# Norm scales applied to products, an earlier start of the recurrence, and tanh gates in a two-block transformer kernel

## Chip, cores and metric

One core of a Trainium2 chip runs the whole program. The metric is the device time of one execution in microseconds (us). The engines are named as in the profile: PE is TensorE, DVE is VectorE, ACT is ScalarE, POOL is GpSimd, SP issues DMAs.

## What is computed

512 tokens of width 1024 pass through a first block (two attentions, gates, an output product `o1`, a final RMS norm) and then a second block of two layers. The change touches the seam of the blocks and layer 0 of the second one:

```python
x = rms_norm(h + merged @ w_out, final_norm_gain)           # end of the first block
h = rms_norm_2(x, mix_norm_g[0]);  z = h @ hg_w_in          # mixer norm, columns q | f | i | g | qm
mem_n = rms_norm_2(mem, mem_norm_g[l])                      # 256 memory rows, l = 0 and 1
kv = mem_n @ w_mem_kv[l];  k = rms_norm_2(kv[..., :256]);  q = rms_norm_2(qm)
m = softmax(q @ k.T * scale) @ kv[..., 256:]                # memory attention, 4 heads
o = hgrn2(q, f, i)                                          # recurrence, 6 heads of 128
o = rms_norm_2(o, onorm_g) * silu(g)                        # per head
x = x + concat([o, m]) @ w_out[0]                           # then the feed-forward of layer 0
```

## The kernel before

The tokens lie along the free axis: `X[:, k, :]` is feature tile k (of 8) for all 512 tokens. Every dense product is split in high and low halves (`XH`, `XL`; weights `WH`, `WL`), three 512-column matmuls for each of 8 k-tiles, 24 for one job. A job is a 128x1024 weight slab or several. The order of jobs is fixed in `plan_stream` (line 90 on) and each engine has its whole program written out in that order, tied by semaphores. A slab goes through three engines: SP brings it to `RAW` (a ring of 4), ACT rounds it to `WH` (`high`, L1104), POOL subtracts to get `WL` (`low`, L541). `WH` and `WL` have two slots (`SPLIT = 2`): `split_past(name)` on ACT issues `high` for the slab two after the named job's, and has to wait until that job is done. Four PSUM banks `DB[0..3]` take the jobs' results in turn, and each is emptied by ACT or DVE, as the plan says.

Around the change the work runs in this order:

- `zb0..7`, `pab0..7`: the gates and branch products. ACT evacuates `zb`, DVE forms the merged tiles `MH`, `ML`.
- `o1_0..7`: the first block's output product. DVE adds each to `X` and squares and sums it (`add_to_x`, L1575 to L1580). Between them memory is loaded to `MRAW` and its norm runs on DVE and ACT (`norm(1, ...)`): 16 tiles of 256 columns are multiplied by gain and root (L1544), rounded (ACT L1143) and subtracted (L1548) into `XH`, `XL`. All of it stands in DVE's order between `o1_3` and `o1_4`.
- `norm_sum(2)`: PE sums the squares of the finished `X`; root; DVE multiplies the 8 tiles of `X` by gain and root (L1763). `norm_sum(3)` and `norm_high(3)` are the mixer norm of the same `X`: squares, root, 8 more tiles of multiply, round and subtract. Memory keys and values (`mk00, mk01, mv0, mk10, mk11, mv1`, 256 columns) are in between.
- `qm00, qm01` (queries of the memory attention), `hf0..5` (forget gates, ACT sigmoid, then a block of six Ln), `hq0..5` (Silu), with the scans of the decays on DVE (L1790, L1791) as soon as the Ln are done.
- Memory attention `m0`: 8 pairs of steps with `hv0`, `hv1` (the values of the recurrence) as pieces beside. DVE makes row minima (L1668), ACT the Exp (L1191), PE transposes, ACT copies to `PT` (L1201), PE multiplies by values.
- The recurrence: for each head h, 7 levels (POOL makes differences L576, L577; ACT Exp L1379; DVE `weigh` L1822; PE L912; DVE `place`), an exact diagonal and two block steps, then PE L939. The job `hg{h}` (the output gate's column tile) is cut in 8 pieces laid beside levels 1 to 8. ACT copies it out (`evac`), and does Silu for four heads after head 4 and for two at the end (`gates_done`, L1369).
- The outputs' RMS norm: squares by ACT (L1361), sums in groups `hoa` (heads 0 to 3) and `hob` (4 and 5), root, `head_spread` by PE (L693), `output_made` and `output_low` by DVE, `output_high` by ACT. Heads 0 to 2 lie within head 5's levels, heads 3 to 5 behind the recurrence, before `wo00`.
- `tail(0, ...)`: `wo00..7` and the feed-forward. Here a norm already goes the other way: `late_tile` (ACT L1148 to L1150) and `late_low` (DVE L1586, L1590) write the halves of the unscaled sum times gain, and the root multiplies products later.

Of the kernel before, what the change touches and what calls it, by code (L numbers as in the profile page):

```python
# [15 lines left out]
P = 128  # L16
# [15 lines left out]
HG = 6  # L32
# [35 lines left out]
def plan_stream():  # L68
# [50 lines left out]
    for k in range(HG):  # L119
        add(f"hg{k}", 1, 1, KD, "act", (0,))  # L120
# [38 lines left out]
SQB = {0: 0, 1: KD, 3: 2 * KD}  # L159
ACC = {0: 0, 1: KD - 1, 2: 2 * (KD - 1), 3: 2 * KD - 1, 4: 3 * KD - 2, 5: 3 * KD - 1, 6: 3 * KD}  # L160

XLB = {0: 0, 1: KD, 3: 3 * KD}
LATE = {4: 0, 5: KD, 6: 2 * KD}


def plan_heads():
# [3 lines left out]
    for group, names, parts, m, nt in (("mk", [f"mk{l}{k}" for l in range(2) for k in range(2)], 1, 2, MEM // P),  # L170
                                       ("qm0", ["qm00", "qm01"], 1, 2, NT), ("hoa", [f"ho{h}" for h in range(4)], 1, 1, NT), ("hob", ["ho4", "ho5"], 1, 1, NT),
# [15 lines left out]
XTB = XLB  # L187
WO0 = [6, 7, 0, 1, 2, 3, 4, 5]
# [10 lines left out]
def build(nc, stream, xt_in, memt_in, pars, convp, consts, rope_tabs, toep, masks8, resets, cz_in, pos_in, out):  # L199
    with ExitStack() as ctx:  # L200
# [62 lines left out]
        MRAW = at("MRAW", [P, KD, MEM], A0 + 0)  # L263
# [62 lines left out]
        SUMS_AT = {"mk": (SC[0], 0), "qm0": (SC[0], 16), "hoa": (TB, 16), "hob": (TB, 32), "cq": (SC[0], 0), "ckv": (SC[0], 4),  # L326
# [45 lines left out]
        x_new = sem("x_new")  # L372
# [47 lines left out]
        hg_silu = sem("hg_silu")  # L420
# [116 lines left out]
        def _(pool):  # L537
# [20 lines left out]
            lows(JOBS["za7"].done + SPLIT, s0 + 2)  # L558

            pool.wait_ge(decays_ready, 1)  # L560
            for h in range(HG):
                b = HB[:, h, :]
                for l in range(8):
# [18 lines left out]
                    if h and l == 1:  # L582
                        low((s0 + h + 1) % RING, s0 + h + 1)
# [5 lines left out]
        def _(pe):  # L589
# [106 lines left out]
            def norm_sum(q, n=TOK):  # L696

                pe.wait_ge(acc_done, ACC[q] + (KD - 1 if q in SQB else 1))
                sum_cols(SC[0], PB[:, 0 if q in SQB else 2, 0:n], ONES[:, 0:1]).then_inc(ss_done, 1)

            def norm_spread(q, n=TOK):
                pe.wait_ge(rs_ready, q + 1)
                spread(SC[1], RS[:, 0:n]).then_inc(rs_spread, 1)
# [51 lines left out]
            def head_sum(group, a, part=0):  # L755
# [7 lines left out]
                sq = (TMP[:, a % 2, :] if group in ("hoa", "hob") else square_at(idx))[:, 0:P * nt]  # L763
# [1445 lines left out]
```

## Time and profile before

| | us |
|---|---|
| median of 3 runs | 1872.19 (1869.97 to 1872.7) |
| profiled execution | 1874.77 |
| its span, first to last instruction | 1873.0 |
| PE busy in it | 1747.3 (93%) |
| DVE / ACT / POOL busy | 893.0 / 760.1 / 699.6 |

The profiled execution is 2.6 us above the median. PEclk is the clock granted to TensorE as a share of 2.4 GHz: 0.50 is 1.2 GHz. A matmul's start is recorded, its end is modelled, so two neighbours overlap in the rows. "idle before" in brackets is the time in which the engine had nothing to do, and what ended it.

### The profile page before, as it was taken

The page shows a single profiled execution, that of the slowest core. Times are in us where ns is not written, and L with a number is a line of the kernel's source. Part 1 is how long each engine was busy: PE and PEld are TensorE (multiplying, and loading weights), DVE is VectorE, ACT ScalarE, POOL GpSimd, SP SyncE. Part 2 cuts the span into 40 slices and gives each one's busy share as a digit, 9 for nine tenths or more (in the row PEclk, how much of TensorE's full clock was granted, in tenths as well). Part 3 has the DMA queues.
Part 4 walks back from the last instruction along what each step waited for, and adds up shares of the span by engine and source line. Part 5 has one row for each costly group of instructions (what it writes and reads, how often), then busy time and mean ns, then how long its engine had stood idle before and what let it go on. Part 6 is the DMA issues. An engine that isn't in the chain of part 4 may idle for free.

```text
span 1873.0 us, 24838 instructions
## 1 busy us (share of the span) xinstructions
PE 1747.3 (93%) x8605; PEld 1420.2 (76%) x8605; DVE 893.0 (48%) x1675; ACT 760.1 (41%) x1167; POOL 699.6 (37%) x362
## 2 busy tenths in 40 slices
PE   5999899998689989889999999998887999999999
PEld 4778566887668778778888888887755788888887
DVE  3587565457534236554555541143454355555200
ACT  4333455323335424444545443324423354444322
POOL 2344211443333346514444444543300244444444
PEclk9999899999789979899999999999988899999999
DMA  4233211232222211012323233332200123332333
GB/s 178 84 108 101 63 40 35 90 111 92 79 67 90 79 45 35 23 34 91 101 90 100 90 101 106 108 96 68 74 5 1 56 91 94 97 101 90 101 106 118
DMA packets 43278, 151.75 MB, mean 81 GB/s; under 512 B 4929, under 2 KB 5057, under 8 KB 43073
## 3 DMA queue, kind: packets, MB, share of 16 engines
q1 hardware_dynamic: 41184, 145.16, 24.7%
q10 hardware_dynamic: 2016, 5.53, 0.9%
q8 instruction: 51, 0.84, 0.2%
q14 instruction: 27, 0.21, 0.0%
HBM read 148.58 MB, written 2.10 MB: 80 GB/s over the span
## 4 chain that ended last, share of the span: by engine, by line
issue 53%; POOL 23%; PE 21%; DVE 1%; ACT 1%; DMA 1%; POOLq 1%; ACTq 0%; DVEq 0%
POOL WL L541 22%; PE DB L617 4%; PE DB L618 3%; PE DB L619 3%; PE SC L912 2%; PE SC L717 1%; PE DB L742 1%; PE OB L731 1%; PE TB L617 1%; PE DB L731 1%; DMA CONST<-in_consts_dram 1%; PE TB L618 0%; PE TB L619 0%; PE DB L669 0%; PE DB L667 0%
## 5 line engine op out<-in xcount | busy, mean ns | idle before, releaser
L541 POOL TENSOR_TENSOR WL<-RAW,WH 128x1024 fp32r<-128x1024 f32 x268 | 643.5, 2401 | 1161.4 <-ACT WH L1104 1161.4
L1104 ACT ACTIVATE WH<-RAW 128x1024 fp32r<-128x1024 f32 x268 | 283.7, 1059 | 731.5 <-PE DB L619 307.0
L617 PE MATMUL DB<-XH,WH 128*128 128x512 f32 (+1 forms) x616 | 256.2, 416 | 11.7 <-DVE XL L1548 6.5
L972 PE MATMUL DB<-XH,WH 128*128 128x512 f32 x640 | 249.0, 389 | 0.0
L973 PE MATMUL DB<-XL,WH 128*128 128x512 f32 x640 | 249.0, 389 | 0.0
L974 PE MATMUL DB<-XH,WL 128*128 128x512 f32 x640 | 249.0, 389 | 0.0
L618 PE MATMUL DB<-XL,WH 128*128 128x512 f32 (+1 forms) x616 | 243.8, 396 | 0.0
L619 PE MATMUL DB<-XH,WL 128*128 128x512 f32 (+1 forms) x616 | 243.1, 395 | 0.0
L617 PEld LDWEIGHTS DB<-XH,WH 128*128 128x128 f32 x616 | 120.6, 196 | 51.0 <-issue 19.1
L619 PEld LDWEIGHTS DB<-XH,WL 128*128 128x128 f32 x616 | 120.6, 196 | 24.9
L972 PEld LDWEIGHTS DB<-XH,WH 128*128 128x128 f32 x640 | 120.1, 188 | 25.1
L973 PEld LDWEIGHTS DB<-XL,WH 128*128 128x128 f32 x640 | 120.1, 188 | 24.9
L974 PEld LDWEIGHTS DB<-XH,WL 128*128 128x128 f32 x640 | 120.1, 188 | 24.8
L991 PE MATMUL DB<-GH,WH 128*128 128x512 f32 x352 | 136.9, 389 | 0.0
L992 PE MATMUL DB<-GL,WH 128*128 128x512 f32 x352 | 136.9, 389 | 0.0
L993 PE MATMUL DB<-GH,WL 128*128 128x512 f32 x352 | 136.9, 389 | 0.0
L618 PEld LDWEIGHTS DB<-XL,WH 128*128 128x128 f32 x616 | 120.9, 196 | 20.5 <-issue 1.2
L1914 DVE TENSOR_TENSOR DB<-DB,SQ 128x512 f32<-128x512 f32 x88 | 61.2, 695 | 42.0 <-PE DB L974 41.2
L993 PEld LDWEIGHTS DB<-GH,WL 128*128 128x128 f32 x352 | 66.1, 188 | 13.7
L991 PEld LDWEIGHTS DB<-GH,WH 128*128 128x128 f32 x352 | 66.1, 188 | 13.7
L992 PEld LDWEIGHTS DB<-GL,WH 128*128 128x128 f32 x352 | 66.1, 188 | 13.6
L1201 ACT ACTIVATE PT<-DB 128x512 f32<-128x512 f32 (+3 forms) x52 | 35.8, 688 | 99.7 <-PE DB L742 99.7
(398 smaller groups left out, 2916.9 us busy)
## 6 DMA issues: line engine op xcount, KB each, us to landing
RAW<-in_stream_dram SPq DMA_DIRECT2D x268, 512.0 KB, 3.5
TP<-in_toep_dram ACTq DMA_DIRECT2D x4, 512.0 KB, 3.7
out_dram<-X SPq DMA_DIRECT2D x8, 256.0 KB, 4.4
X<-in_xt_dram SPq DMA_DIRECT2D x4, 256.0 KB, 5.2
X<-in_xt_dram ACTq DMA_DIRECT2D x4, 256.0 KB, 5.6
MRAW<-in_memt_dram ACTq DMA_DIRECT2D x1, 1024.0 KB, 6.2
CONST<-in_consts_dram ACTq DMA_DIRECT2D x1, 448.0 KB, 9.9
MSKI<-in_masks_dram ACTq DMA_DIRECT2D x1, 288.0 KB, 3.5
```

The costliest lines, as they stand in the source:

```text
L541: nc.gpsimd.tensor_tensor(WL[:, s, :], RAW[:, j, :], WH[:, s, :].bitcast(F32), ALU.subtract).then_inc(lo_done, 1)
L617: mm(o, WH[:, s, c], hi(k), start=(k == 0), stop=False)
L618: mm(o, WH[:, s, c], lo(k), start=False, stop=False)
L619: last = mm(o, WL[:, s, c], hi(k), start=False, stop=(k == job.kts - 1))
L972: mm(o, WH[:, s, c], xh(k), start=(k == 0), stop=False)
L973: mm(o, WH[:, s, c], xl(k), start=False, stop=False)
L974: last = mm(o, WL[:, s, c], xh(k), start=False, stop=(k == KD - 1))
L991: mm(o, WH[:, s, c], GH[:, k, :], start=(k == 0), stop=False)
L992: mm(o, WH[:, s, c], GL[:, k, :], start=False, stop=False)
L993: last = mm(o, WL[:, s, c], GH[:, k, :], start=False, stop=(k == FF - 1))
L1104: A(WH[:, n % SPLIT, :], RAW[:, n % RING, :], ACT.Copy).then_inc(hi_done, 1)
L1914: V.tensor_tensor(DB[j], DB[j], SQ[:, 0, :], ALU.mult).then_inc(scaled, 1)
```

## The change

1. The final norm, the mixer norm and the memory norms no longer multiply tiles. Memory (`MRAW`, now in the space of `SB` and `PT`) is loaded at the end of the first attention, and squared and summed during `zb`/`pab`. Its halves `MXH`, `MXL` (own space) are memory times gain, without the root, and are made between the `o1` jobs. The keys take the root in DVE (`ROOTM`), the values in ACT's evacuation as a scale.
2. `o1` jobs end in `late_tile`/`late_low` with gain `GAIN2` (final gain times mixer gain): per tile 4 ACT instructions, a DVE addition, a DVE subtract and two DVE additions into `TB` and `OB` (two sums of squares). The roots of both norms are formed from the two sums with a chain of small instructions; `ROOT2` multiplies each product of `qm`, `hf`, `hq`, `hg` on DVE in its bank (`root_scaled`); the values take it as a scale.
3. The scan of head k stands behind `root_scaled("hq{k}")` on DVE; ACT's Silu of `hq` waits for it too. The fill of `PT`, the `decays_ready` signal and POOL's first levels come before or inside the memory attention; the first Exp of head 0 stands in ACT's order just before the last copy to `PT` (`values_and_first_level`). The last group of memory outputs is left for DVE to finish within head 0.
4. The gate is `tanh(0.5 z)` on ACT, and `(tanh + 1) * z` on DVE, one head later; the factor 0.5 is in the norm's gain. Pieces of `hg` lie beside levels 2, 3, 4, 5, 6, 7, 7, 8.
5. Output norms in three groups: heads 0 to 2, 3 and 4, and 5. `wo00` and `wo01` are run in pieces, with the spreads and sums of heads 3 to 5 between the pieces.

The diff, cut to its core ("..." marks what is left out):

```diff
-XLB = {0: 0, 1: KD, 3: 3 * KD}
-LATE = {4: 0, 5: KD, 6: 2 * KD}
+LATE = {2: 0, 4: KD, 5: 2 * KD, 6: 3 * KD}
+SPREAD_AT = [(4, 6), (5, 3), (5, 8)]
+GATE_AT = [2, 3, 4, 5, 6, 7, 7, 8]
...
             pool.wait_ge(decays_ready, 1)
+            pool.wait_ge(exp_done, segments["m0"][-1][1]["g"] + 1)
...
-                    if h and l == 1:
-                        low((s0 + h + 1) % RING, s0 + h + 1)
+                    if l == 1:
+                        low((s0 + h + (h > 0)) % RING, s0 + h + (h > 0))
+                    if h == 0 and l == 4:
+                        low((s0 + 1) % RING, s0 + 1)
...
             for k in range(2):
                 feature_job(f"mk0{k}", *memory_halves(0), n=MEM, xready=XLB[1])
+            norm_sum(2)
+            norm_sum(3)
             token_job("mv0", *memory_halves(0), MEM, tiles=2)
...
+            pe.wait_ge(std_done, 4)
+            for a in range(2):
+                head_sum("mk", a)
             token_job("mv1", *memory_halves(1), MEM, tiles=2)
             pe.drain().then_inc(arena_free, 1)
-            pe.wait_ge(x_new, KD)
+            norm_spread(2)
             norm_spread(3)
...
+                if final is not None:
+                    A(PB[:, b % 2, :], DB[b][:, :], ACT.Square, scale=final)
+                    A(flat(X[:, dk, :]), DB[b][:, :], ACT.Identity, scale=final).then_inc(x_back, 1)
...
+            def values_and_first_level():
+                act.wait_ge(slab_used, JOBS["hv1"].done)
+                values(1)
+                act.wait_ge(act_emptied, EMPTIED[JOBS["hv1"].banks[-1]][1])
+                act.wait_ge(lv_e, 1)
+                A(EX[0][:, :], SB[:, 0, :], ACT.Exp).then_inc(lv_x, 1)
...
-            def gates_done(a, b):
-                A(HGT[:, a:b, :], HGT[:, a:b, :], ACT.Silu).then_inc(hg_silu, 1)
+            def gate_tanh(h):
+                A(HGT[:, h, :], DB[JOBS[f"hg{h}"].bank()], ACT.Tanh, scale=0.5).then_inc(hg_tanh, 1)
...
             for k in range(HG):
+                root_scaled(f"hq{k}")
                 dve.wait_ge(hf_ln, k + 1)
                 link(V.tensor_scalar(HK[:, k, :], HK[:, k, :], LBC[:, 18 + k:19 + k], None, ALU.mult))
                 link(V.tensor_tensor_scan(HB[:, k, :], RESET[:, :], HB[:, k, :], 0.0, ALU.mult, ALU.add))
             link(V.tensor_copy(MSK[:, :], MSKI[:, :]))
-            attention(segments["m0"])
-            V.memset(PT[:, :, :], 0.0)
+            link(V.memset(PT[:, 1, :], 0.0))
             V.drain().then_inc(decays_ready, 1)
+            memory_out = attention(segments["m0"], keep=True)
```

## Rows read from the trace of the kernel before

**Rows 1.** the page: its first line, and the busy time of the engines.

```profile
span 1873.0 us, 24838 instructions
PE 1747.3 (93%) x8605; PEld 1420.2 (76%) x8605; DVE 893.0 (48%) x1675; ACT 760.1 (41%) x1167; POOL 699.6 (37%) x362
```

**Rows 2.** stretches: length, busy PE, PEld, DVE, ACT, POOL (instructions), granted clock, DMA.

```profile
416.84:521.58 104.74, 78.25 (x424) 68.45 (x425) 68.55 (x92) 36.24 (x63) 40.90 (x17) 0.88 0.31 100
521.58:617.51 95.93, 90.14 (x400) 72.37 (x400) 32.83 (x40) 40.79 (x57) 31.76 (x13) 0.95 0.24 72
617.51:671.70 54.19, 49.24 (x321) 42.11 (x320) 15.48 (x66) 23.48 (x54) 16.65 (x7) 1.00 0.23 77
671.70:679.37 7.67, 0.00 (x0) 0.03 (x1) 2.98 (x4) 3.67 (x8) 7.36 (x7) 0.67 0.36 109
679.37:706.96 27.59, 27.07 (x120) 24.79 (x121) 12.36 (x23) 6.94 (x12) 11.02 (x16) 0.60 0.02 9
706.96:725.42 18.46, 17.68 (x130) 16.12 (x129) 12.11 (x23) 7.72 (x13) 11.66 (x17) 1.00 0.09 29
762.33:814.66 52.33, 42.36 (x282) 37.78 (x281) 30.55 (x57) 24.20 (x34) 21.42 (x29) 0.90 0.07 21
814.66:823.64 8.98, 5.54 (x35) 5.27 (x33) 4.39 (x8) 3.58 (x6) 0.00 (x0) 0.67 0.20 58
829.64:862.28 32.64, 32.64 (x146) 27.03 (x144) 12.34 (x18) 15.67 (x24) 14.39 (x6) 1.00 0.28 82
511.02:513.98 2.96, 2.96 (x25) 2.96 (x25) 0.00 (x0) 0.78 (x3) 2.40 (x1) 1.00 0.50 169
```

**Rows 3.** waits of PE from 416.84 to 829.64: waited for, total, times, longest.

```profile
PE SC L686 <- DVE PB L1580: 14.7, 1, 14.7
```

**Rows 4.** the same view as rows 2, for three short stretches.

```profile
469.60:490.10 20.50, 7.55 (x35) 7.49 (x36) 14.88 (x21) 2.34 (x5) 2.34 (x1) 0.50 0.10 36
...
674.40:701.70 27.30, 22.33 (x85) 20.43 (x86) 10.62 (x20) 5.36 (x9) 13.87 (x20) 0.50 0.12 39
...
645.00:648.40 3.40, 0.96 (x7) 0.58 (x6) 1.53 (x8) 3.40 (x10) 0.98 (x1) 1.00 0.40 142
```

**Rows 5.** timeline while PE runs `wo03`; columns start, duration, engine, line.

```profile
840.72 1.06 ACT L1104 ACTIVATE WH<-RAW 128x1024 fp32r<-128x1024 f32 x1 [2.83 <-PE DB L619]
...
841.86 2.40 POOL L541 TENSOR_TENSOR WL<-RAW,WH 128x1024 fp32r<-128x1024 f32 x1 [3.05 <-ACT WH L1104]
...
842.26 0.59 ACT L1149 ACTIVATE SQ<-DB 128x512 f32<-128x512 f32 x1
...
843.36 0.75 DVE L1586 SCALAR_TENSOR_TENSOR XL<-DB,PAR,XH 128x512 fp32r<-128x512 f32 x1 [1.95 <-ACT X L1150]
```

**Rows 6.** DVE instructions by line: duration ns min/median/max, first and last start.

```profile
L1721 DVE SCALAR_TENSOR_TENSOR MB<-SB,IW,MB x9: 483/752/2022, 72.9 to 105.2; 128x256 f32<-128x256 f32 x3, 128x384 f32<-128x384 f32 x3, 128x512 f32<-128x512 f32 x3
...
L1791 DVE TENSOR_TENSOR_SCAN HB<-RESET,HB x6: 1223/1224/3393, 588.5 to 601.5; 128x512 f32<-128x512 f32 x6
...
L1792 DVE CAST MSK<-MSKI x1: 2476/2476/2476, 602.7 to 602.7; 128x576 int8<-128x576 int32 x1
```

**Rows 7.** timeline at the start of the memory attention.

```profile
618.34 0.42 DVE L1668 CUSTOM_DVE_ANT_0 SB<-SC,CZ 128x256 f32<-128x256 f32 x1 [13.13 <-PE SC L717]
...
618.75 2.35 POOL L541 TENSOR_TENSOR WL<-RAW,WH 128x1024 fp32r<-128x1024 f32 x1 [3.04 <-ACT WH L1104]
```

**Rows 8.** timeline between the memory attention and head 0.

```profile
672.01 4.65 POOL L541 TENSOR_TENSOR WL<-RAW,WH 128x1024 fp32r<-128x1024 f32 x2 [7.34 <-ACT WH L1104]
...
672.78 1.62 ACT L1119 ACTIVATE HV<-DB 128x384 f32<-128x384 f32 x4
```

**Rows 9.** timeline at the start of head 1.

```profile
704.84 2.36 POOL L541 TENSOR_TENSOR WL<-RAW,WH 128x1024 fp32r<-128x1024 f32 x1 [12.89 <-ACT WH L1104]
...
709.88 0.85 PE L912 MATMUL SC<-PB 128*128 128x64 f32 x6 [0.27 <-DVE PB L1822]
```

**Rows 10.** ACT's timeline between heads 4 and 5.

```profile
780.67 1.28 ACT L1369 ACT_TABLE_LOAD   x1
```

More of the change, by code:

```diff
@@ L334, in square_at, with memory @@
             return (SQ[:, 0, :], SQ[:, 1, :], PB[:, 0, :], PB[:, 1, :])[(idx - QN0) % 4]
+        GAIN2 = LBC[:, 8:16]
+        def memory(k):
+            return MRAW[k // 4][:, k % 4, :]
         def flat(t):
@@ L940, in _, with output_ready, tail @@
                 last.then_inc(ho_mm, 1)
-            pe.wait_ge(hs_done, HEADS["ho2"][0] + 1)
-            head_spread("ho3", DB[1])
-            head_sum("hob", 1)
-            head_spread("ho4", DB[2])
-            head_spread("ho5", DB[3])
-            def tail(l, hi, lo, ni, inputs):
-                for k in range(KD):
+            def output_ready(j):
+                return (hs_done, HEADS[f"ho{WO0[j]}"][0] + 1) if WO0[j] < HG else (o_out, WO0[j] + 3)
+            first, second = (feature_tiles(f"wo0{k}", lambda j: YH[:, WO0[j], :],
+                                           lambda j: YL[:, YLSLOT[WO0[j]], :] if WO0[j] < HG else YLM[:, WO0[j] - HG, :],
+                                           inputs=output_ready) for k in range(2))
+            for _ in range(2):
+                next(first)
+            head_spread("ho3", DB[2])
+            head_spread("ho4", DB[3])
+            for _ in range(3):
+                next(first)
+            pe.wait_ge(hs_std, HEADS["ho4"][0] + 1)
+            head_sum("hoc", 0)
+            for _ in range(5):
+                next(second)
+            head_spread("ho5", SC[0])
+            for _ in itertools.chain(first, second):
+                pass
+            def tail(l, hi, lo, ni, inputs, jobs=range(KD)):
+                for k in jobs:
                     feature_job(f"wo{l}{k}", hi, lo, inputs=inputs if k == 0 else None)
@@ L1179, in group_std, with attention @@
                   bias=col("eps", eps)).then_inc(hs_std, len(names))
-            def attention(seg, after=None):
+            def attention(seg, after=None, ending=None):
                 n = len(seg)
                 for k in range(n + 1):
+                    if k == n and ending is not None:
+                        ending()
                     if k < n:
@@ L1299, in _ @@
-            mixer_squares(0, 1)
-            evac("mk00", MKT[0][:, 0, :], width=MEM)
-            mixer_squares(2, 3)
-            evac("mk01", MKT[0][:, 1, :], width=MEM)
-            mixer_squares(4, 5)
+                if k == 0:
+                    act.wait_ge(mem_in, 32)
+                if k >= 3:
+                    act.wait_ge(acc_done, ACC[1] + k - 2)
+                A(PB[:, 1, MEM * (k % 2):MEM * (k % 2) + MEM] if k else PB[:, 0, 0:MEM], memory(k), ACT.Square).then_inc(sq_done, 1)
@@ L1678, in attention @@
                             leaving.pop(0)
-                for group in leaving:
+                for group in () if keep else leaving:
                     for _ in group:
@@ L1683, in attention @@
                 dve.wait_ge(tr_done, seg[-1][0]["g"] // 2 + 1)
+                return itertools.chain(*leaving)
             x_norm(0, "norm_gain")
@@ L1781, in _ @@
                 head_copy("qm0", k)
+            root_scaled("hf3")
             for k in range(2):
```

368 lines of the change are left out of this document (226 added, 142 removed).

## Prediction

> **What bounds the kernel now.** I read the page's busy times first [rows 1]: PE is busy 1747.3 of 1873.0 us, so only idle or slow PE time can be won. The change adds next to nothing to PE and takes next to nothing away; what counts is which waits of PE it removes or makes. Then the stretches [rows 2], cut at job borders of PE: `o1_0` to `qm00` (416.84 to 521.58), `qm00` to `hq5` (to 617.51), the memory attention (to 671.70), an empty stretch (to 679.37), head 0 (to 706.96), one undisturbed head (to 725.42), heads 4 and 5 (762.33 to 814.66), and the way to `wo00` (to 823.64). Two rows say what undisturbed work costs: six jobs in 32.64 us, so 5.44 us for a job, and 2.96 us for a 256-column job. Last, which wait ends the holes: the longest is 14.7 us, PE's column sums waiting for DVE's sum of squares [rows 3].
>
> The granted clock is the second cost. It is 0.50 (1.2 GHz) from 469.6 to 490.1, three microseconds into that long wait and nine past its end, and from 674.4 to 701.7, which begins in the empty stretch and lasts through most of head 0 [rows 4]. Head 0 takes 27.59 us at 0.60, head 1 18.46 us at 1.00, for the same work [rows 2]. So a hole costs its length and then some; but a shorter one need not, since 645.0 to 648.4 has PE busy for 0.96 of 3.40 us at clock 1.00 [rows 4].
>
> I work from each stretch's "work at full clock": busy time, less half of what was busy at the low clock.
>
> **1. From `o1_0` to `qm00`: minus 26.5 us.** PE is busy 78.25 of 104.74 us at mean clock 0.88, so some 25 us at half clock; 7.55 busy in the 20.5 of rows 4, nearly all in the other 4.6, which makes 12.2 and a loss of 6.1. Work at full clock: 72.2 us. The change takes out of DVE's order the 32 memory instructions and the 23 of `add_to_x` that made the 14.7 us [rows 3], and the 8 scalings of `X` and the second norm's 16 that stand before `qm00`. In their place each `o1` has on ACT `high` (1.06), four passes (0.59 each, overlapping to 0.5 or so) and up to three memory tiles (some 0.4 each): 4.5 us of 5.44. On DVE: a subtract of 0.75, three additions at or a little below that, three memory subtracts of half the width, some 0.4: 4.1 us [rows 5]. The trap is that DVE instructions with only SBUF operands wait out a POOL `low`: L1721, the same instruction kind, takes 483 at best and 2022 ns at worst [rows 6]. The memory subtracts sit exactly where POOL runs its 2.40 us [rows 5]; I price that as up to 1.6 us of lag for `o1_0..4`, caught up in `o1_5..7`, which have one memory subtract or none. PSUM-sourced ones are not held up.
>
> Behind `o1_7` the chain to the sums (high, four passes, three DVE, two copies) is some 6.5 us, and `mk00`, `mk01` give 5.9 us of cover. New waits: the slab path (1.06 + 2.40 and two signals, 3.8 us) is longer than a 2.96 us job, 0.8 us for each of the 8 slabs if nothing else is between; the sums of `mk` on PE need squares that ACT makes only behind the `high` of `mk11`, 1.6 us; the small root chain is covered by `mv0` and `mk1`. Bounds: 0 to 12 us. I take 5, plus 1 us for two key sums that moved in. 72.2 + 6 = 78.2, against 104.74.
>
> **2. From `qm00` to `hq5`: minus 8.6 us.** Busy 90.14 of 95.93 at 0.95: 9.6 us at half clock, a loss of 4.7, work 85.4 us. `qm00` no longer waits for its halves tile by tile. One us of sums has moved away; what stays is one us of waiting in the spreads of `mk` and a late slab for `hq2`: behind `hf5` come the scaling 0.7, `high` 1.06, two sigmoids 1.1, a table load 1.28, six Ln 4.3, `high` again 1.06, `low` 2.40 and some signals, 12.8 us at most against two jobs, 10.9; I take 1.9 [rows 5, 10]. 87.3 against 95.93. The scalings of `hf`, `hq` (0.7 us each on DVE in 5.44) are free; their cover is the job itself.
>
> **3. Start of the memory attention: plus 9 us.** This is where the change loses. DVE now does after the last `hq5` matmul: scaling 0.7, HK 0.5, scan 1.22, mask copy, `PT` fill and a drain, and only then the first row minimum, which now starts 0.83 us after the job (618.34) [rows 7]. POOL's `low` begins 1.24 us after the job [rows 7] and the scan and the copy are SBUF-only: 1224 ns against 3393, and 2476 ns, where they met it [rows 6]. So: scaling to 0.85, HK to 1.4, scan held to 3.6 and done at 4.8, copy 0.6, fill 0.5, rest 0.2: first minimum at 6.2 instead of 0.83, 5.4 us later. Queued behind it are both first row minima, ACT's Exp and PE's third scores with all pieces of `hv0`. A hole of six us should lower the clock as the others did; I price 3.5 us. Bounds 2.5 (no collision, no slow clock) to 13.
>
> The Trainium skill (SBUF — State Buffer, "SBUF: two separate sides") says that VectorE and GpSimd hold a shared port pair exclusively, for a whole instruction, when a VectorE instruction has two SBUF inputs or a double-port mode. The trace agrees (3393 against 1224 ns); without that rule this part would be 2.2 us less.
>
> **4. Attention's end and head 0: minus 13.5 us.** Now 35.3 us from 671.70 to 706.96. POOL first does two slabs, 4.65 us, and then the levels [rows 8]; ACT evacuates the values, 1.62 us. After: level 0 waits for nothing but Exp, which stands in ACT's order behind the values and before the last `PT` copy. That copy comes some 1.9 us later than PE wants it, so the last product ends 1.1 us later than now, and head 0 follows at once. At full clock head 0 is 18.45, plus 0.8 (part 5), plus 1.3 for DVE's fill and the memory outputs (1.4 us) and a slab on POOL among the levels: 20.5. 21.6 against 35.3. Bounds: 19.5, and 31 if the clock stays low.
>
> **5. Heads 1 to 3: plus 2.8 us.** At a head's start POOL does the next gate slab for 2.36 us, then level 2, and PE gets level 2 at 709.88, five us after that slab began [rows 9]. The gate piece that lay before this wait (an eighth of a job and a restart, 0.8 us) has moved behind level 7, where PE had no room; DVE's `(tanh + 1) * z` adds 0.15. So 0.95 us a head; the bounds are 0 and 1.5 (both DVE instructions uncovered).
>
> **6. Heads 4 and 5: minus 4.5 us.** 52.33 us now, against 2 x 18.45 + 3 spreads of 0.9 = 39.6 undisturbed. Between them ACT loads three tables at 1.28 us [rows 10], with a root and four Silu. After: one root within head 4 with two loads, 1.5 us on PE; copies and outputs on DVE, 2; part 5's 1.9; in head 5 the output steps, 2.5. 47.8 with rounding; bounds 43 to 54.
>
> **7. The way to `wo00`: minus 3.3 us.** 8.98 us with PE busy 5.54 at 0.67 goes; 2.4 us of spreads and sums return among the pieces, 1.4 of waiting for head 5's halves, and 1.5 for `wo02`'s slab, whose slot is freed only when `wo00` ends, one job before it is needed, not two.
>
> **Sum:** -26.5 - 8.6 + 9 - 13.5 + 2.8 - 4.5 - 3.3 = -44.6. The profiled execution would be 1874.8 - 44.6 = 1830.2; the median is 2.6 less: 1828 us (rounded).
>
> **Rivals.**
> (a) The clock stays low through head 0. For it: 27.3 us at 0.50 behind the present hole [rows 4]; the new hole is 1.9 us, but level 2 adds another. Against: 645.0 to 648.4. Plus 9: 1837.
> (b) The attention starts without collision and without slow clock, minus 6.5: 1821. For it: the scan's median is 1224 ns [rows 6].
> (c) The `o1` chain doesn't keep up: DVE's lag doesn't shrink, the sums find nothing ready, a hole of 4 us lowers the clock again, and each short slab costs its 0.8. Plus 14: 1842. For it: ACT at 4.5 of 5.44 with a root and a table load in `o1_0`. Against: ACT's third pass ends 2.6 us after `high` starts [rows 5].
> (d) Tanh isn't in the Exp table: two loads a head, 2.56 us on ACT where it is waited for from level 2 on, of which 0.4 are slack; some 1.2 for each of five heads, plus 6: 1834. Rows 10 show only that Silu isn't. The Trainium skill (ScalarE: Activation LUTs, "Table sets: the hidden batching unit") lists tanh in exp's set, so no load; no row of before shows a tanh.
> (e) The other side: PE's longer pause before level 2 (1.1 us, now 0.27) in each head, after a hole, keeps the clock at 0.50 for the whole recurrence. Each head then costs 27.6 instead of 18.45, as head 0 does now. Six heads at 9.1, less 3.5 that heads 4 and 5 lose already, is plus 51: 1879. It decides from five slow heads on. Against: the heads from 1 on stand at 1.00 with three pauses each.
>
> **How the numbers follow.** Forecast 0.43 (1818 to 1838 by itself); (a) 0.18, (b) 0.12, (c) 0.13, (d) 0.04, (e) 0.05 (0.04 slower, 0.01 even); (a) with (c), at 1851, 0.05. The likeliest is 1828. 1809 to 1851 leaves out (e), half of the last and the tails, under 2 in 10. A measurement tells about 0.2%, 3.7 us, from no change. Faster 0.95, same 0.01, slower 0.04.
>
> **What would show it.** Right: no wait over 2 us before the sums of norm 2; `qm00` within 77 to 80 us of `o1_0`; a hole of 4 to 7 us after the first scores of the memory attention with a scan over 3 us before it; under 3 us before head 0; PE idle about 1.1 us before each level 2; no table load in heads 1 to 3. Wrong: a clock of 0.50 in heads 1 to 3, a DVE that starts an `o1` addition more than 2 us after its job, or a hole before `wo02` over 3 us.

## The result

| | before | after |
|---|---|---|
| median | 1872.45 us (1869.97 to 1874.48, 4 runs) | 1852.16 us (1850.68 to 1853.26, 4 runs) |
| span of the profiled execution | 1873.0 us | 1850.0 us |
| ratio | | 0.9887 [0.9868, 0.9905] |

The change is 20 us faster. The forecast was 1828, with a range from 1809 to 1851: the direction was right, the size less than half of what was forecast, and the time one us above the range. First lines of the page of the profile after, to set against [rows 1]: PE is as busy as before in a span 23 us shorter.

```profile
span 1850.0 us, 24845 instructions
PE 1750.2 (95%) x8605; PEld 1427.9 (77%) x8605; DVE 898.4 (49%) x1689; ACT 762.8 (41%) x1174; POOL 699.3 (38%) x362
```

The stretches of the profile after, cut at the same job borders as [rows 2] and with its columns (length, busy PE, PEld, DVE, ACT, POOL, granted clock, DMA): `o1_0` to `qm00`, to the end of `hq5`, memory attention, from there to the end of head 0, head 1, heads 2 and 3, heads 4 and 5, the way to `wo02`, the rest.

```profile
415.48:495.82 80.34, 76.74 (x433) 67.55 (x433) 49.28 (x74) 46.62 (x77) 39.05 (x17) 0.96 0.36 111
495.82:581.97 86.15, 83.62 (x396) 69.28 (x394) 40.53 (x46) 35.02 (x47) 32.78 (x14) 1.00 0.29 86
581.97:647.70 65.73, 53.89 (x321) 46.12 (x320) 21.02 (x72) 27.30 (x60) 22.48 (x14) 0.90 0.23 71
647.70:672.71 25.01, 22.17 (x120) 20.60 (x121) 15.49 (x28) 7.79 (x12) 12.69 (x16) 0.73 0.07 22
672.71:691.86 19.15, 17.61 (x130) 16.27 (x129) 13.28 (x24) 7.74 (x13) 11.67 (x17) 1.00 0.08 29
691.86:734.94 43.08, 40.00 (x258) 36.73 (x257) 26.30 (x48) 16.33 (x26) 23.33 (x33) 0.88 0.09 25
734.94:787.80 52.86, 47.85 (x282) 43.94 (x280) 31.59 (x58) 18.89 (x31) 21.41 (x29) 0.81 0.07 21
787.80:808.20 20.40, 15.25 (x81) 12.46 (x81) 11.11 (x20) 7.36 (x14) 2.40 (x2) 1.00 0.08 27
808.20:1850.00 1041.80, 1004.96 (x4633) 825.22 (x4633) 443.91 (x765) 424.54 (x573) 404.03 (x168) 0.97 0.28 86
```

Part by part, before against after, with what was forecast:

| part | before | after | change | forecast |
|---|---|---|---|---|
| ahead of `o1_0` | 416.84 | 415.48 | -1.4 | 0 |
| 1. `o1_0` to `qm00` | 104.74 | 80.34 | -24.4 | -26.5 |
| 2. `qm00` to `hq5` | 95.93 | 86.15 | -9.8 | -8.6 |
| 3. memory attention | 54.19 | 65.73 | +11.5 | +9 |
| 4. its end and head 0 | 35.3 | 25.0 | -10.3 | -13.5 |
| 5. heads 1 to 3 | 55.4 | 62.2 | +6.9 | +2.8 |
| 6. heads 4 and 5 | 52.3 | 52.9 | +0.5 | -4.5 |
| 7. way to `wo02` | 20.4 | 20.4 | 0 | -3.3 |
| the rest | 1037.9 | 1041.8 | +3.9 | 0 |

Parts 1 and 2 won about what they were to win. The rows behind them share one column: the clock is 1.00 only in head 1 and on the way to `wo02`, where before it was 1.00 in the memory attention and in every head from 1 to 3. Spells at 0.50 (1.2 GHz) stand at 586.7 (10.2 us long), 620.9 (3.4), 648.2 (13.7), 696.0 (3.4), 716.4 (6.8), 740.3 (17.1) and 767.6 (3.4).

Each begins within a hole of PE or up to 1.6 us behind one. (A hole is idle time of PE between two matmuls, a spell a stretch at 0.50.) Part 1 has two spells too, of 3.4 us each, while PE is busy. The first has no hole near it: the last one, of 0.79 us, ended 6 us before. In the columns of the stretches:

```profile
470.70:474.10 3.40, 3.40 (x18) 3.40 (x18) 1.73 (x5) 0.30 (x1) 0.61 (x1) 0.50 0.69 233
487.70:491.10 3.40, 3.40 (x19) 3.40 (x18) 0.00 (x0) 0.22 (x1) 0.00 (x0) 0.51 0.56 171
```

The start of the memory attention went as the working said. This is the timeline (start, duration, engine, line, idle before): the scan held to 3.36 us beside POOL's `low`, the first row minimum 6.25 us after the job, where it was 0.83 before [rows 7], and PE's third scores after a hole of 6.38 us.

```profile
583.21 2.34 POOL L556 TENSOR_TENSOR WL<-RAW,WH 128x1024 fp32r<-128x1024 f32 x1 [3.04 <-ACT WH L1143]
583.26 3.36 DVE L1900 TENSOR_TENSOR_SCAN HB<-RESET,HB 128x512 f32<-128x512 f32 x1
...
588.22 0.43 DVE L1721 CUSTOM_DVE_ANT_0 SB<-SC,CZ 128x256 f32<-128x256 f32 x1 [0.25 <-DVE LBC L1903]
...
589.05 1.23 PE L741 MATMUL SC<-MKT,QM 64*128 64x256 f32 x4 [6.38 <-DVE ST L1721]
```

The end of the memory attention, in the timelines of PE, DVE and ACT. PE's last product waits 2.06 us for the `PT` copy, behind the values and head 0's Exp, as forecast (1.9). Level 0 doesn't follow at once, though: DVE first empties `OB` in two steps of 0.69, and only then begins level 0's product at 649.19. The diff says that this last group of memory outputs is left for head 0, but in DVE's program the loop that empties ready groups runs once more after the last pair, so the group isn't left.

```profile
647.04 0.66 PE L755 MATMUL OB<-PT,MVT 128*64 128x128 f32 x8 [2.06 <-ACT PT L1248]
650.03 1.30 PE L937 MATMUL SC<-PB 128*128 128x64 f32 x5 [2.33 <-DVE PB L1937]
...
647.74 0.69 DVE L1686 CAST YH<-OB 128x512 fp32r<-128x512 f32 x1 [11.14 <-PE OB L755]
648.47 0.69 DVE L1689 TENSOR_TENSOR YLM<-OB,YH 128x512 fp32r<-128x512 f32 x1
649.19 1.29 DVE L1937 TENSOR_TENSOR PB<-HKQ,DB 128x512 f32<-128x512 f32 x2
...
643.84 2.00 ACT L1388 ACTIVATE HV<-DB,ST 128x384 f32<-128x384 f32 x4 [3.58 <-PE DB L687]
```

In each head PE stands before its third level (level 2 of the prediction). That pause was 0.27 [rows 9] and is 1.02 us in heads 1, 2, 3 and 5; in head 4 it is 1.86, since ACT makes the root of heads 0 to 2 there with a table load on either side. PE's and ACT's timelines:

```profile
675.63 0.74 PE L937 MATMUL SC<-PB 128*128 128x64 f32 x5 [1.02 <-DVE PB L1937]
...
738.70 1.08 PE L937 MATMUL SC<-PB 128*128 128x64 f32 x8 [1.86 <-DVE PB L1937]
...
733.76 1.28 ACT L1223 ACT_TABLE_LOAD   x1
735.06 0.27 ACT L1223 ACTIVATE HR<-TB,PAR 128x12 f32<-128x12 f32 x1
735.35 1.28 ACT L1429 ACT_TABLE_LOAD   x1
```

From 600 to 820 us there are three table loads, two here and one at 786.61, all at a root: a tanh between two Exp brings none, as the Trainium skill (ScalarE: Activation LUTs, "Table sets: the hidden batching unit"), cited with rival (d), has it.

On the way to `wo02` PE's waits (waited for, total, times, longest) are three:

```profile
PE DB L635 <- DVE HGT L1909: 1.9, 1, 1.9
PE DB L635 <- POOL WL L556: 1.6, 1, 1.6
PE DB L635 <- DVE YL L1920: 1.6, 1, 1.6
```

The last two are the forecast's waits for head 5's halves and `wo02`'s slab (1.4 and 1.5). The first isn't in the forecast: `wo00`'s bank is the one from which DVE multiplies head 5's gate, and in DVE's order this product stands behind the wait for the last root.

### The profile page after: what moved, and what is told of

It is laid out like the page before. It is cut to its first block, busy times and chain, and to the rows that moved or that the text cites. A ratio compares the mean times of both kernels' runs of the same rounds, so it can differ in the third digit from the quotient of the medians.

```text
span 1850.0 us, 24845 instructions
## 1 busy us (share of the span) xinstructions
PE 1750.2 (95%) x8605; PEld 1427.9 (77%) x8605; DVE 898.4 (49%) x1689; ACT 762.8 (41%) x1174; POOL 699.3 (38%) x362
## 4 chain that ended last, share of the span: by engine, by line
issue 49%; PE 25%; POOL 22%; DVE 2%; ACT 1%; DMA 1%; POOLq 0%; ACTq 0%; DVEq 0%
POOL WL L556 21%; PE DB L635 4%; PE DB L636 4%; PE DB L637 4%; PE SC L937 2%; PE SC L741 2%; PE DB L766 1%; PE DB L685 1%; PE DB L686 1%; PE DB L687 1%; PE OB L755 1%; PE TB L635 1%; PE DB L755 1%; DMA CONST<-in_consts_dram 1%; PE TB L636 0%
## 5 line engine op out<-in xcount | busy, mean ns | idle before, releaser
L635 PE MATMUL DB<-XH,WH 128*128 128x512 f32 x584 | 244.0, 418 | 5.4 <-DVE XL L1610 3.2
L1011 PE MATMUL DB<-XH,WH 128*128 128x512 f32 x640 | 249.0, 389 | 0.0
L1012 PE MATMUL DB<-XL,WH 128*128 128x512 f32 x640 | 249.0, 389 | 0.0
L1013 PE MATMUL DB<-XH,WL 128*128 128x512 f32 x640 | 249.0, 389 | 0.0
L636 PE MATMUL DB<-XL,WH 128*128 128x512 f32 x584 | 232.5, 398 | 0.0
L637 PE MATMUL DB<-XH,WL 128*128 128x512 f32 x584 | 232.0, 397 | 0.0
L635 PEld LDWEIGHTS DB<-XH,WH 128*128 128x128 f32 x584 | 112.6, 193 | 41.7 <-issue 14.9
L1013 PEld LDWEIGHTS DB<-XH,WL 128*128 128x128 f32 x640 | 120.1, 188 | 25.1
L1012 PEld LDWEIGHTS DB<-XL,WH 128*128 128x128 f32 x640 | 120.1, 188 | 24.9
L1011 PEld LDWEIGHTS DB<-XH,WH 128*128 128x128 f32 x640 | 120.1, 188 | 24.8
L637 PEld LDWEIGHTS DB<-XH,WL 128*128 128x128 f32 x584 | 112.6, 193 | 24.9
L636 PEld LDWEIGHTS DB<-XL,WH 128*128 128x128 f32 x584 | 112.9, 193 | 21.0 <-issue 1.2
L1032 PEld LDWEIGHTS DB<-GH,WL 128*128 128x128 f32 x352 | 66.1, 188 | 13.7
L1031 PEld LDWEIGHTS DB<-GL,WH 128*128 128x128 f32 x352 | 66.1, 188 | 13.7
```

What stands on the lines that cost most here:

```text
L635: mm(o, WH[:, s, c], hi(k), start=(k == 0), stop=False)
L636: mm(o, WH[:, s, c], lo(k), start=False, stop=False)
L637: last = mm(o, WL[:, s, c], hi(k), start=False, stop=(k == job.kts - 1))
L1011: mm(o, WH[:, s, c], xh(k), start=(k == 0), stop=False)
L1012: mm(o, WH[:, s, c], xl(k), start=False, stop=False)
L1013: last = mm(o, WL[:, s, c], xh(k), start=False, stop=(k == KD - 1))
```

## The experiments

The theory after this reading: what is missing is clock. Pauses of 1 to 2 us in every head, and the holes at the attention's two ends, lower it. In the expectations the start of wo02, behind which the rest is measured, is by mistake that of `wo03`, one job of 5.5 us further; the stretches from there are 1036.3 us after and 1032.5 before.

**Gate pieces back at level 1.**

```diff
-        add(f"hg{k}", 1, 1, KD, "dve", (0,))
+        add(f"hg{k}", 1, 1, KD, "dve", (1,) if k in (1, 3) else (0,))
...
-                    for _ in range(GATE_AT.count(l)):
+                    for _ in range((list(range(1, 9)) if 1 <= h <= 4 else GATE_AT).count(l)):
```

> The changed kernel, but for heads 1 to 4 the gate piece lies again beside level 1 (pieces beside levels 1 to 8), and hg1, hg3 use bank DB[1] so that the piece needn't wait for DVE's gate of the head before. PE's work is the same. Theory A: PE's pause of 1.02 us before level 2 is what lowers the clock in heads 2 to 4 (0.50 at 696.0, 716.4 and 740.3 of the changed kernel's trace, each within 2 us of that pause). Then the pause is about 0.3 us, heads 1 to 3 come to 18.5 us each (now 19.15, 20.74, 22.34: 62.2 together, to 55.5) and head 4 loses 3 to 6 us of its 28.9: the time falls by 8 to 13 us, to 1840 to 1844. Rival B: the slow clock in these heads has nothing to do with the piece (the recurrence's small matmuls, or chance). Then only the 0.7 us a head comes back, 3 us in all: 1849.

Measured: 0.9786 [0.977, 0.9803], span 1830.5. Head 1 and head 4 (with the columns above):

```profile
671.21:689.67 18.46, 17.68 (x131) 16.12 (x129) 13.27 (x24) 7.75 (x13) 11.66 (x17) 1.00 0.10 30
726.58:751.54 24.96, 22.03 (x138) 20.00 (x137) 16.95 (x31) 10.40 (x18) 12.10 (x17) 0.86 0.06 22
```

Heads 1 to 3 take 18.46, 18.45 and 18.46 us, as before the change (head 1 in [rows 2]). So the move of the piece is the whole loss of part 5, and it costs more than the pause: head 1 pays 0.7 us for it, the three together 6.9.

**The same pause filled with work that nobody reads**, which moves none of the kernel's own work:

```diff
                     if l == 0:
                         gate = feature_tiles(f"hg{h}", xh, xl)
+                    if l == 1 and 1 <= h <= 4:
+                        mm(DB[1], IDENT, HV[:, 0, 0:TOK], start=True, stop=True)
```

> The changed kernel with one extra 128x128 by 128x512 f32 matmul into an unused bank beside level 1 of heads 1 to 4, in the pause before level 2; nothing is moved, and its result isn't read. It takes some 0.9 us, so the pause of 1.02 us is filled by useless work. Theory A (the pause lowers the clock): heads 1 to 3 keep 19.2 us each at clock 1.00 and the time falls by 5 to 10 us, to 1842 to 1847, although PE does more. Rival B (the pause doesn't matter to the clock): no gain, or 1 to 2 us slower where the extra matmul runs past the pause, 1852 to 1854.

Measured: 0.9806 [0.9788, 0.9823], span 1835.5. Head 1 and head 4, and last, for comparison, head 4 of the changed kernel:

```profile
671.52:690.65 19.13, 18.51 (x132) 16.49 (x131) 13.27 (x24) 7.75 (x13) 11.64 (x17) 1.00 0.09 29
...
728.91:751.26 22.35, 19.65 (x140) 17.32 (x139) 17.01 (x31) 10.42 (x18) 12.04 (x17) 1.00 0.08 25
...
734.94:763.86 28.92, 26.54 (x138) 24.53 (x137) 16.39 (x31) 10.40 (x18) 11.87 (x17) 0.70 0.07 19
```

Three heads at 19.13 and head 4 at 22.35 instead of 28.92, at clock 1.00 throughout. Level 2 comes no earlier, 2.91 us after the start of head 1 against 2.92; PE is merely busy while it waits. This parts the two costs: the pause itself is 0.7 us a head (0.95 was forecast), and the clock takes 4.8 us in heads 1 to 3 and 6.6 in head 4. The spell in head 4 is no accident of one trace: all nine traces in which the gate pieces lie as in the changed kernel and nothing fills the pause have it, with 17.1 or 20.5 us.

**Scans one slot earlier on DVE**, with the mask copy and the fill behind `hq3` and `hq4`:

```diff
             for k in range(HG):
                 root_scaled(f"hq{k}")
-                dve.wait_ge(hf_ln, k + 1)
...
+                for a in ((0,), (1, 2), (3, 4), (5,), (), ())[k]:
+                    decays(a)
```

> The changed kernel, but DVE makes the scans one behind hq0, two behind hq1 and hq2, one behind hq3, and the mask copy and fill before hq5, so that only hq5's scaling stands between its job and the first row minimum. Theory: the 6.38 us hole at the start of the memory attention (PE, 582.7 to 589.05) is DVE's queue of scan, copy and fill, held up by POOL's slab. It should fall to some 1.5 us, as before the change, and the slow clock at 586.7 to 596.9 should go: 6 to 9 us less, 1843 to 1846. Rival: ACT's Silu and its table load for Exp (some 3 us behind the job) end last once DVE is free, so that the hole falls only to 3 or 4 us, and the clock still drops: 2 to 4 us less.

Measured: 0.9812 [0.9795, 0.9828], span 1837.6. DVE now has only a scaling between `hq5` and the first minimum; the second row is the whole memory attention, in the columns of the stretches.

```profile
582.81 0.70 DVE L1867 TENSOR_TENSOR DB<-DB,ROOT 128x512 f32<-128x512 f32 x1 [3.80 <-PE DB L637]
583.44 0.42 DVE L1721 CUSTOM_DVE_ANT_0 SB<-SC,CZ 128x256 f32<-128x256 f32 x1
...
582.70:638.25 55.55, 49.23 (x321) 42.09 (x320) 16.13 (x67) 27.20 (x60) 22.52 (x14) 1.00 0.27 84
```

65.73 has become 55.55 us, at clock 1.00: DVE's scan, mask copy and fill behind `hq5` were 10 of the 11.5 us of part 3. What is left over the 54.19 of before is the later `PT` copy.

**The last memory group really left for head 0.**

```diff
+                    if keep and k == n + 3:
+                        continue
+
                     while leaving and kind(leaving[0]) == "m":
```

> The changed kernel, but the last group of memory outputs is really left for head 0: in the trace of the changed kernel DVE makes them at 647.74, before it weighs level 0 at 649.19, since the loop over the leaving groups empties them although keep is set. Theory: the 2.33 us hole before level 0 goes to under 0.5 us; if the clock then stays at 1.00, head 0 falls from 22.7 to 20 us, together 5 us less, 1847. Rival: the hole of 2.06 us before the last product (values and Exp ahead of the last copy to PT) alone lowers the clock; then 1.5 to 2.5 us less, 1850.

Measured: 0.9867 [0.9847, 0.9886], span 1850.7. PE's timeline, and head 0 as a stretch:

```profile
647.63 0.66 PE L755 MATMUL OB<-PT,MVT 128*64 128x128 f32 x8 [2.05 <-ACT PT L1248]
648.22 2.00 PE L937 MATMUL SC<-PB 128*128 128x64 f32 x11
...
648.22:671.79 23.57, 23.05 (x123) 21.30 (x121) 14.73 (x27) 7.57 (x12) 12.70 (x16) 0.71 0.08 23
```

The hole of 2.33 is gone and level 0 follows at once, but behind the 2.05 us before it the clock is at 0.50 for the same 13.7 us, as the rival has it. The stretch is 23.57 us long where it was 25.01: 1.4 us are gained in place of the 5 of the theory. Head 1 then had a spell that it didn't have (20.73), so nothing is left of it.

**Head 5's gate ahead of the last root.**

```diff
-            gate(HG - 1)
             output_low(2, DB[1])
...
+            gate(HG - 1)
             group_roots("hob")
```

> One step moved: DVE multiplies head 5's gate before it waits for the root of the last group of output norms, not behind it. wo00's result bank is the one that this gate product reads, and the changed kernel shows PE idle for 1.95 us at the end of head 5 until that product is there. Theory: the bank is what makes part 7 of the prediction come out at 0 instead of minus 3.3. The idle time goes, and the way from the end of head 5 to wo02 (20.46 us in the changed kernel) takes 18.5 to 19.0 us; the time falls by some 1.5 to 2 us, to a ratio of 0.988 where the changed kernel had 0.9887. Rival: the halves of the late heads set this stretch. Then the idle time only moves behind the first pieces of wo00, the holes of 1.56 and 1.64 us further on grow by as much, the stretch stays at 20.4 us and the time where it was.

Measured: 0.985 [0.9818, 0.9881], span 1841.2. The gate product and the stretch from head 5 to `wo02`:

```profile
785.55 0.69 DVE L1909 SCALAR_TENSOR_TENSOR HGT<-HGT,DB 128x512 f32<-128x512 f32 x1 [0.66 <-ACT HGT L1429]
...
786.59:804.93 18.34, 15.17 (x83) 12.43 (x82) 10.52 (x19) 7.49 (x14) 2.39 (x2) 1.00 0.08 29
```

20.4 has become 18.34 us; the bank was the missing term of part 7. The profiled execution is 8.8 us shorter, though (7 us by the ratios, whose intervals overlap), and the theory gave it 2. The rest is in places that the edit doesn't touch: 5.6 us are behind the start of `wo03`, where the spells at 0.50 sum to 44.4 us instead of 61.4, and 1.2 ahead of head 0. So this gain is mostly clock. Whether the moved product brings it about by moving what follows, no run shows.

**The four edits together.**

> Four edits together: gate pieces beside level 1 (e1), scans one slot earlier (e3), the last memory group really left for head 0 (e4), head 5's gate product ahead of the last root (e5). Theory: they act in different stretches and add up. The changed kernel would be at 1854 us beside this chip's 1875; minus 19.6 (e1), minus 10 (the memory attention's part of e3), minus 2 (the start of head 0), minus 1.5: 1821 us, ratio 0.971, with heads 1 to 3 at 18.5 us each, the memory attention at 55 us and the stretch from head 5 to wo02 at 19 us. Rival: what one edit wins the next one has to wait for, above all at the seam of memory attention and head 0, where the clock stays at 0.50 for 10 to 14 us whatever comes before. Then head 0 takes 23 us or more and the ratio is 0.975 or above.

Measured: 1820.87 us, 0.9729 [0.9706, 0.9753], span 1814.0. Head 0, and head 4:

```profile
641.66:660.30 18.64, 17.30 (x123) 15.33 (x122) 15.07 (x27) 7.57 (x12) 13.27 (x16) 1.00 0.09 29
...
715.66:737.40 21.74, 18.81 (x139) 16.94 (x138) 16.96 (x31) 10.41 (x18) 12.12 (x17) 1.00 0.08 25
```

They add up, and the median is the 1821 us of the theory. That it fits to the us is luck: the four executions lie between 1815.8 and 1825.1 us. Head 0 runs at 1.00 although the same hole of 2.06 us stands before it.

**The order at the seam turned round**: the `PT` copy first, then the values and head 0's Exp (the two lines that call `ending` move below the copy).

> Alone on the changed kernel: ACT makes the last copy to PT before it evacuates the values and makes head 0's first Exp, not behind them. PE's last products of the memory attention then wait some 0.6 us instead of 2.06, and level 0 of head 0 waits for the Exp, some 2 us, so that one hole replaces another. Theory: the clock falls there because PE has by then lost about 4 us of 6 in two holes and two small transposes, wherever they lie; the 0.50 spell of 13.7 us stays at 10 us or more, head 0 begins 0.5 to 1 us earlier, and the time is within 1.5 us of the changed kernel (ratio 0.988). Rival: the first hole (2.06 us before the last products) is what lowers it, as the kernel with the last group left for head 0 suggests. Then head 0 runs at 1.00 and the time falls by 3 to 4 us, to a ratio of 0.9865 or below.

Measured: 0.9853 [0.9834, 0.9873], span 1839.1. The seam and head 0:

```profile
645.14:648.18 3.04, 0.27 (x7) 0.06 (x3) 2.22 (x4) 2.56 (x6) 0.89 (x2) 0.90 0.26 104
648.18:669.84 21.66, 21.14 (x121) 19.60 (x122) 13.26 (x25) 7.71 (x12) 12.90 (x16) 0.78 0.08 25
```

A hole of 0.69 and one of 2.77 in place of 2.06 and 2.33, and a spell of 10.2 us: on the spell the theory was right. On the time it was wrong, which fell by some 7 us, about twice what even the rival gave. The profiled execution is 10.9 us shorter, of which 1.9 lie between the last transposes of the memory attention and the end of head 0. Of the rest, 3.2 are in heads 2 and 3, with one short spell between them (19.13 and 20.73), and 3.1 behind the start of `wo03` (1033.1 us).

**Both holes at the seam filled**, on top of the four edits:

```diff
+                    if k == n + 2 and pieces == 2 and not banks_read:
+                        for _ in range(2):
+                            mm(SC[1][:, :], IDENT, X[:, 0, 0:TOK], start=True, stop=True)
...
             n = 0
+            for _ in range(2):
+                mm(SC[1][:, :], IDENT, X[:, 0, 0:TOK], start=True, stop=True)
```

> The kernel with four edits (e6), and PE does work whose result nobody reads: two 128x512 products into a score bank before the last products of the memory attention, and two more before level 0 of head 0, 1.2 us at full clock for each pair. Theory: the holes at this seam are what puts the clock at 0.50 through head 0. With them filled, head 0 takes 18.5 to 20 us instead of 22 to 23.5, and the kernel is 2.5 to 4 us faster than e6. Rival: the spell comes from thin work before the holes as well (pieces of hv1 with waits between), so it only moves or shortens a little: within 1 us of e6, or slower by the 1.2 us that the second pair may cost.

Measured: 1822.02 us, 0.9718 [0.9692, 0.9743], span 1821.2. Head 0 takes 18.16 us at 1.00, a little under the theory's 18.5 to 20. But the kernel with four edits had no slow head 0 in its profile either, and the total is the same within the spread of the runs. So this experiment doesn't show that the filled holes keep the clock up.

**The untouched rest.** Three kernels on one chip: the changed one again, the same with sixteen products that nobody reads ahead of `cq0`, and the one with four edits again.

```diff
+            for _ in range(16):
+                mm(TB[:, 0:P], IDENT, IDENT, start=True, stop=True)
             feature_job("cq0", xh, xl, inputs=lambda j: emptied(f"dn0{j}", dve_emptied))
```

> The changed kernel itself, unaltered, timed again beside the next two. Earlier single edits moved the time by more than the stretch they touch: the one with head 5's gate moved was 10 us faster by its median, of which its own stretch explains 2.2. Behind the start of wo02 every kernel does the same work, and ten traces show it taking 1029.1 to 1037.9 us, longer by 0.37 us for each us that the clock stands at 0.50 in it (41 to 65 us). Theory: the same holes lower the clock or don't, by where they happen to fall, so the changed kernel's own ratio moves by some tenths of a per cent from chip to chip and its runs spread by several us: 0.986 to 0.990 here, single runs 5 us or more apart. Rival: it is steady at 0.9887 within 0.1%, and the moved gate is worth 10 us by some way that its trace doesn't show.

> Sixteen 128x128 products, 1.7 us, whose result nobody reads, are put ahead of the first product of layer 1, at about 1190 us; all else is the changed kernel. Layer 1 then does the same work 1.7 us later. Theory: where its holes fall decides on the clock, so the time from wo02 to the end changes by something else than 1.7 us: between 3 us less and 6 us more than that, and the sum of spells at 0.50 in it isn't the 61.4 us that the changed kernel, the one with the earlier scans and the one with the kept group have. Rival: the holes' lengths alone decide; then the spells stay where they are with respect to the holes, their sum stays 61.4 us, and the stretch takes 1036.3 plus 1.7, 1038.0 us, within 0.5.

> The kernel with four edits (e6), unaltered, beside the changed kernel on one chip. Theory: both carry the same scatter from layer 1, so the difference between them stays near the one found across chips, 1.5 to 1.8% (27 to 33 us), and of it 8 to 9 us are the memory attention, 15 to 20 us are heads 1 to 5, 2 us the start of head 0 and its slow clock 3 to 4. Rival: part of the difference was the luck of one profile and one chip; then it shrinks to 20 us or less.

Measured: the changed kernel 1852.09 us (1851.92 to 1853.32), 0.9884 [0.9864, 0.9905]; with the shift 1855.05, 0.9902 [0.9877, 0.9926]; four edits 1819.88, 0.9706 [0.9678, 0.9734]. The changed kernel is steady within 1.4 us, as the first half of the rival has it. It is 32.2 us above the one with four edits on the same chip, within the 27 to 33 that the theory gave. The one with four edits isn't: single runs lie between 1813.2 and 1824.8, and its second profile, of the very same program, shows head 0 and head 4 like this, where the first had 18.64 and 21.74 at 1.00:

```profile
638.51:658.87 20.36, 19.84 (x123) 18.42 (x122) 14.76 (x27) 7.58 (x12) 12.73 (x16) 0.83 0.08 27
...
714.23:740.72 26.49, 23.63 (x139) 21.39 (x137) 16.87 (x31) 10.41 (x18) 12.04 (x17) 0.81 0.06 21
```

The sixteen products took 3.5 us, twice what I had worked out, and everything behind them came 3.5 us later with nothing else changed: this test spoke for the rival, whose 1038.0 becomes 1039.8 with the true length, against 1039.9 measured. So two smaller shifts were tried, by the same edit with eight and with four products.

> Eight idle products ahead of layer 1 instead of sixteen. The sixteen ran as 32 instructions and took 3.5 us, not 1.7, and the stretch from wo02 to the end grew by 3.5 us, with each spell at 0.50 moved by the same amount and their sum unchanged at 61.4 us. So eight shift layer 1 by 1.75 us. Theory: where the holes fall decides on the clock, and a shift of 3.5 us happened to put them where they were before; a shift of half of it doesn't. The sum of spells at 0.50 behind wo02 then leaves 61.4 us (41 to 55, as in the kernels that had another offset), and the stretch takes 1031 to 1036 us in spite of the added 1.75. Rival: the holes' lengths and the work around them alone decide, so the sum stays 61.4 us and the stretch takes 1036.3 plus 1.75, 1038.1 us, within 0.5.

> Four idle products, a shift of 0.9 us. Theory: again another sum of spells at 0.50 than 61.4 us, with the stretch from wo02 to the end anywhere from 1030 to 1038 us, and not 0.9 above the changed kernel's. Rival: 61.4 us and 1036.3 plus 0.9, 1037.2 us, within 0.5.

Measured: with eight 1853.97 us (1853.58 to 1856.94), 0.9888 [0.9872, 0.9905]; with four 1849.63 us (1849.18 to 1850.13), 0.9865 [0.9849, 0.9881]. The stretch from `wo03` to the end in the changed kernel, with four products, with eight, and in the kernel with the gate pieces at level 1:

```profile
813.74:1850.00 1036.26, 999.42 (x4610) 820.64 (x4608) 441.61 (x761) 422.88 (x570) 401.65 (x167) 0.97 0.28 85
...
815.15:1848.30 1033.15, 996.83 (x4618) 818.06 (x4616) 441.48 (x761) 422.75 (x570) 401.25 (x167) 0.97 0.28 85
...
815.29:1855.10 1039.81, 1003.27 (x4626) 824.17 (x4624) 441.49 (x761) 423.01 (x570) 401.70 (x167) 0.97 0.27 85
...
801.37:1830.50 1029.13, 991.97 (x4610) 814.36 (x4608) 441.61 (x761) 422.86 (x570) 401.29 (x167) 0.98 0.28 86
```

Adding some 0.9 us of work makes the stretch 3.1 us shorter; adding some 1.75 makes it 3.5 longer (both lengths worked out from the 3.5 us of sixteen). PE's longest waits there, the first row after and the second with four products (whose lines stand two further down), are the same in all of them:

```profile
PE OB L755 <- DVE YL L1689: 10.8, 3, 4.3
...
PE OB L755 <- DVE YL L1691: 10.8, 3, 4.3
```

Only the sum of the spells at 0.50 differs: 61.4 us in the changed kernel, 51.2 with four products, 64.9 with eight, 41.0 in the last, and 51.2 before the change. So the lengths of the holes alone don't decide, and the rival falls: with four products its 1037.2 is missed by 4 us. The theory's forecast was no better with eight, where it gave 1031 to 1036. What is shown is that a small shift of the same work changes how long the clock is low; by how much, and which way, neither side could forecast.

## Why the prediction was wrong

**Parts 1 and 2** came close: 80.34 against 78.2 forecast, 86.15 against 87.3. In part 1 the forecast's waits stand there, 1.5 us for the sums of `mk` and 0.8 for a short slab twice. But its closeness is in part luck. PE's idle time is 3.6 us where 5 were taken for waits, and the low clock, for which this part had nothing, takes 3.4 (half of the two spells, in which PE is busy throughout).

**Part 3** was right in its mechanism and nearly in its size (+11.5; of it 1.4 are the late `PT` copy, a hole of 2.06 us for one of 0.69, which the forecast had put into part 4 with 1.1; so +10.1 against +9). The first minimum came 6.25 us after the job (forecast 6.2). The clock took 4.7 us where 3.5 were priced: PE was busy for 53.89 us, and for 49.23 with the same work at 1.00 in the kernel with earlier scans.

**Part 4** failed in two sentences. "Head 0 follows at once": it followed 2.33 us later, because the last group isn't left (read from the diff's `keep=True`, not from the loop). And the clock: rival (a) came true by half, with 13.7 us at 0.50 where it had 27.3. Head 0 took 22.7 us where it takes 18.64 at 1.00.

**Part 5** named the pause (1.1 us forecast, 1.02 measured) and priced it as 0.95 us a head (0.7 measured). The failed step, here and in parts 4 and 6, is that nothing was added for the clock, while rival (e) added it for all six heads. Both treated it as all or nothing. It is neither: spells of 0, 3.4 and 6.8 us in heads 1 to 3, 4.8 us in all.

**Part 6.** The largest single miss. The root within head 4 was priced at 1.5 us on PE. Its pause of 1.86 lowers the clock for 17.1 us, which is 6.6 us; without that, heads 4 and 5 take some 46.3 us, below the 47.8 of the forecast. The size is uncertain: with the gate piece back at level 1 and the root where it was, head 4 has a spell of 6.8 us in one trace (24.96 us), of 10.2 in another (26.49), and none in a third (21.74) of the same program as the second.

**Part 7** missed the bank: the first wait above is 1.9 of the 3.3 us. The spreads and sums among the pieces are 3.3 us long, not 2.4.

**The rest**, +3.9, was no step of the prediction. It is the clock again, in the same work at another moment.

Put together by cause: between forecast (-44.6) and measurement (-23.0) lie 21.6 us. The clock takes 3.4 (part 1), 1.2 (part 3), 4.0 (head 0), 4.8 (heads 1 to 3), 6.6 (head 4) and 3.9 (the rest), 23.9 in all; the other misses cancel but for 2.3 the other way. Shown by an experiment are those of heads 1 to 4 (the filled pause) and the rest's dependence on a shift. Head 0's is the difference between two kernels, and part 1's is half the time of its spells, whose cause stays open. The prediction's own sum has slips: the terms written under parts 4, 6 and 7 give -13.7, -4.8 and -3.7 instead of -13.5, -4.5 and -3.3. That would have made 1827 of 1828 and explains nothing. Against the clock the forecast cited one hole, 645.0 to 648.4 at 1.00 [rows 4]. The hole was real. One case isn't a price.

## What to carry to other kernels

When a change gives a loop a pause, price it twice: the time itself, and the chance that the clock falls behind it. A piece of other work laid into the pause is worth more than its own length: here 6.9 us in three heads for pieces of 0.8 us each, and even a product that nobody reads brought 4.8 of them. Judge a small edit by its own stretch in the trace, not by the whole kernel's time: a kernel with many holes can move by 3 to 9 us in places that the edit doesn't touch, as three kernels here did. The version to keep is the one with four edits, at 0.9706 to 0.9729 of before and 32 us under the changed kernel on the same chip.

## What the runs showed that was not expected

Whether the clock falls behind a hole isn't settled by the hole. I counted PE's holes between 500 and 1460 us in all fifteen traces, where the clock was 1.00 before, and asked whether a spell at 0.50 begins about the hole (from 1 us ahead of it to 5 us behind it):

| length of the hole, us | holes | followed by 0.50 |
|---|---|---|
| 0.9 to 1.25 | 76 | 29 |
| 1.25 to 1.75 | 103 | 44 |
| 1.75 to 2.25 | 64 | 46 |
| 2.25 to 2.75 | 55 | 43 |
| over 2.75 | 59 | 59 |

The kernels are nearly alike, so most of these holes are the same place counted many times. Of the 202 spells that begin in this range, 7 have no hole of 0.9 us or more about their start, all at one place of the second layer.

The work around a hole has its part too (those on the way to `wo02`, 1.56 and 1.64 us with long products on either side, had none behind them in any trace), so this is a count, not a law. But it could have been made on the trace of before alone, where 7 of 9 holes from 1.75 to 2.75 us were followed by a fall, and would have made rival (a) likelier than the forecast. The same hole of 2.06 us before the same products was followed by a fall in one execution of the kernel with four edits and not in another. The Trainium skill (TensorE: Matmul & The Clock Gate, "Part 1: The HAM clock gate") calls the monitor behind the clock free-running, so that where it stands differs from run to run. The two profiles of one program agree with that; the changed kernel's own steadiness, 1.4 us over five runs, doesn't follow from it, and stays open.

Also, one DVE instruction with a single SBUF tensor and a column was held as the scan was: the decay's multiply took 2.10 us beside a `low` in the kernel with earlier scans, and 0.48 elsewhere.
